# A fused two-block model in fp32: norm sums folded on the way, later tables, and low parts of the normalised tiles made on GpSimd

## What is computed

```python
def rms_norm(x, g):
    y = x * rsqrt(mean(x * x, axis=-1) + EPS)
    return y * g

for l in range(2):                                   # first block
    proj = rms_norm(x, attn_norm[l]) @ w_in[l]
    # three attentions: latent (MLA), differential, chunked
    x = x + concat([o_mla, o_diff, o_ch]) @ w_out[l]
    x = x + conv_ffn(rms_norm(x, ffn_norm[l]), ...)
x = rms_norm(x, final_norm)
h = rms_norm(x, norm_mix_g_2)                        # second block
q, k, v, f, u_ssm, g_attn, g_ssm = split(h @ w_in_2)
x = x + (sigmoid(g_attn) * (y_attn @ w_proj_attn)
         + sigmoid(g_ssm) * (y_ssm @ w_proj_ssm)) @ w_out_2
x = x + hier_moe(rms_norm(x, norm_ffn_g_2), ...)     # 32 experts, two per token
```

## Time and profile before

| | us |
|---|---|
| median of 3 runs | 2308.18 |
| the profiled execution | 2307.2 |
| its span, first to last instruction | 2305.5 |
| PE busy | 2092.2 (91%) |
| DVE busy | 1146.7 (50%) |
| ACT busy | 691.7 (30%) |
| POOL busy | 736.3 (32%) |
| granted TensorE clock, mean share of full speed | 0.965 |

### The profile page before, as it was taken

How to read it: one execution, slowest core, us unless ns; L and a number is a source line. 1 busy time by engine, 2 the same in 40 slices (tenths; PEclk the granted TensorE clock), 3 DMA queues, 4 the chain that set the end, 5 groups by cost and what they waited for, 6 DMA issues and landing times.

```text
span 2305.5 us, 25218 instructions
## 1 busy us (share of the span) xinstructions
PE 2092.2 (91%) x8540; PEld 1339.8 (58%) x8541; DVE 1146.7 (50%) x1929; ACT 691.7 (30%) x1229; POOL 736.3 (32%) x1218
## 2 busy tenths in 40 slices
PE   4999889999797999989999799899998899788795
PEld 3874468888585884466888586346333446333233
DVE  7346756666734436757666833136782522211113
ACT  3227723333412316734333412131000501111010
POOL 4006766656100005766665300001562000111110
PEclk9999999999998999999999999899999998899998
DMA  4210122332232210122323223122321053699984
GB/s 148 92 49 1 37 92 88 113 109 97 70 101 101 92 67 1 38 78 80 117 100 109 72 88 105 37 74 91 110 106 69 27 219 142 243 423 424 425 334 163
DMA packets 43826, 284.19 MB, mean 123 GB/s; under 512 B 8346, under 2 KB 8602, under 8 KB 21072
## 3 DMA queue, kind: packets, MB, share of 16 engines
q1 hardware_dynamic: 33840, 254.34, 29.4%
q0 software_dynamic: 9024, 19.08, 2.2%
q10 hardware_dynamic: 864, 9.44, 1.0%
HBM read 272.68 MB, written 23.60 MB: 129 GB/s over the span
## 4 chain that ended last, share of the span: by engine, by line
PE 77%; DVE 10%; DMA 7%; ACT 3%; POOL 2%; issue 2%; SPq 0%; DVEq 0%; POOLq 0%; ACTq 0%
PE bank L755 10%; PE bank L756 10%; PE bank L757 10%; DMA experts<-in_experts 6%; PE bank L1005 5%; PE bank L1179 4%; PE bank L939 3%; PE bank L940 3%; PE bank L941 3%; PE bank L975 2%; PE bank L1110 2%; PE bank L875 2%; PE bank L742 2%; PE bank L846 2%; PE bank L1182 2%
## 5 line engine op out<-in xcount | busy, mean ns | idle before, releaser
L755 PE MATMUL bank<-h_high,w_high 128*128 128x512 f32 x1056 | 417.7, 396 | 44.5 <-ACT h_high L1426 20.4
L756 PE MATMUL bank<-h_low,w_high 128*128 128x512 f32 x1056 | 415.7, 394 | 0.0
L757 PE MATMUL bank<-h_high,w_low 128*128 128x512 f32 x1056 | 415.5, 393 | 0.0
L1416 ACT ACTIVATE w_high<-extra 128x2048 fp32r<-128x2048 f32 (+1 forms) x104 | 180.5, 1736 | 376.9 <-DVE w_low L1795 376.9
L1792 DVE TENSOR_SCALAR extra<-ring 128x2048 int32<-128x2048 int32 (+1 forms) x104 | 117.8, 1133 | 308.0 <-PE bank L757 182.6
L755 PEld LDWEIGHTS bank<-h_high,w_high 128*128 128x128 f32 x1056 | 201.6, 191 | 94.0 <-issue 36.0
L756 PEld LDWEIGHTS bank<-h_low,w_high 128*128 128x128 f32 x1056 | 201.6, 191 | 41.9
L757 PEld LDWEIGHTS bank<-h_high,w_low 128*128 128x128 f32 x1056 | 201.1, 190 | 42.4
L1795 DVE TENSOR_TENSOR w_low<-ring,extra 128x2048 fp32r<-128x2048 f32 (+1 forms) x104 | 218.6, 2102 | 3.6
L1179 PE MATMUL bank<-experts,rstd 128*64 128x512 f32 x512 | 126.9, 653 | 28.4 <-DMA experts<-in_experts 27.8
L940 PE MATMUL bank<-act_low,w_high 128*128 128x512 f32 x352 | 139.4, 396 | 0.0
(11 more groups left out here) (390 smaller groups left out, 3704.5 us busy)
## 6 DMA issues: line engine op xcount, KB each, us to landing
experts<-in_experts SPq DMA_DIRECT2D x34, 2048.0 KB, 23.5
ring<-in_w_ffn_in SPq DMA_DIRECT2D x44, 1024.0 KB, 4.8
experts<-in_experts SPq DMA_DIRECT2D x34, 1024.0 KB, 21.8
ring<-in_w_ffn_out SPq DMA_DIRECT2D x32, 704.0 KB, 4.1
ring<-in_w_feature SPq DMA_DIRECT2D x14, 1024.0 KB, 4.8
ring<-in_w_rest SPq DMA_DIRECT2D x9, 1024.0 KB, 4.8
ring<-in_w_out SPq DMA_DIRECT2D x8, 1024.0 KB, 4.9
powers_d<-work POOLq DMA_DIRECT2D x16, 512.0 KB, 3.1
```

Source lines behind the costliest of these rows:

```text
L755: pe.matmul(dst, high[:, at], h_high[:, k, :], start=k == 0, stop=False)
L756: pe.matmul(dst, high[:, at], h_low[:, k, :], start=False, stop=False)
L757: return pe.matmul(dst, low[:, at], h_high[:, k, :], start=False, stop=k == KD - 1)
L1416: act.activation(w_high[par_][:, 0:words], w_part[par_][:, 0:words], ACT.Copy).then_inc(w_split, 1)
```

## The change

1. **Sums on the way.** `norm_sum` is one pair of matmuls instead of eight (except for the first norm of all). ACT squares tile m as soon as it has its sum x (`square`), and DVE adds the squares into one tile (`add_square`), during the loop over m of `w_out`, `ffn_out` and `w_out2`.
2. **One seam instead of two at the end of the first block.** The final norm and the norm behind it are computed from two sums, of x^2 and (gain x)^2, taken together; h gets both gains at once, x is multiplied afterwards.
3. **Earlier splits.** The first weight block of the next product is split during the last tiles of the one before (`split_proj(0, l + 1)`, `split(0, 0)`, `split_high(SPLITS, 0)`), and in layer 1 SP loads par and the first weights without waiting for `layer_end`.
4. **Start.** x comes in four parts with four semaphores, weights directly behind it; con2 and rel come later. The S5 angles, sines, factors and the distances move into the feature products of layer 0.
5. **GpSimd.** `lower_tiles` does the subtractions of `split_tile`, 24 in a layer, and stands ahead of the other work of the layer for the first eight, and behind `scale_probs` for the other sixteen; the power tables begin only behind those. The first powers (`first_powers`) come behind the first eight.

```diff
+            def lower_tiles(at):
+                for k in range(KD):
+                    pool.wait_ge(h_masked, at + (k + 1))
+                    pool.tensor_tensor(h_low[:, k, :], h[:, k, :], h_part[:, k, :], ALU.subtract).then_inc(h_lowered, 1)
+                pool.wait_ge(h_lowered, at + KD)
+
             for l in range(LAYERS):
+                lower_tiles(l * (3 * KD))
+                if l == 0:
+                    first_powers()
                 pool.wait_ge(layer_end, l + 1)
...
                 for t in range(NPB):
                     scale_probs(l, t)
+                lower_tiles(l * (3 * KD) + KD)
+                lower_tiles(l * (3 * KD) + 2 * KD)
                 with pool.Fori(l * (ST // LAYERS), (l + 1) * (ST // LAYERS)) as st:
                     power_table(st)
...
                 def split_tile(i, k):
 
-                    at = l * (3 * KD) + (i * KD + k + 1)
                     dve.tensor_scalar(h_part[:, k, :].bitcast(I32), h[:, k, :].bitcast(I32), HIGH_BITS, None, ALU.bitwise_and)\
                        .then_inc(h_masked, 1)
-                    dve.wait_ge(h_masked, at)
-                    dve.tensor_tensor(h_low[:, k, :], h[:, k, :], h_part[:, k, :], ALU.subtract).then_inc(h_lowered, 1)
...
-            sp.dma_start(con2[:], a["con2"]).then_inc(con_in, 16)
...
-            sp.dma_start(x[:], a["x"]).then_inc(x_in, 16)
+            for n in range(X_PARTS):
+                k = KD // X_PARTS
+                sp.dma_start(x[:, n * k:(n + 1) * k, :], a["x"][:, n * k:(n + 1) * k, :]).then_inc(x_in[n], 16)
...
             for l in range(LAYERS):
 
-                sp.wait_ge(layer_end, l + 1)
+                if l:
+                    sp.wait_ge(ffn_act, l * JF)
                 sp.dma_start(par[:], a["par"][l]).then_inc(par_in, 16)
-                sp.dma_start(rel[:], a["rel"][l]).then_inc(par_in, 16)
-                for n in range(FEATURE_BLOCKS):
+                for n in range(RING):
+                    load(l, n, a["w_feature"][l * FEATURE_BLOCKS + n])
+                if l == 0:
+                    sp.dma_start(con2[:], a["con2"]).then_inc(con2_in, 16)
+                sp.dma_start(rel[:], a["rel"][l]).then_inc(rel_in, 16)
+                for n in range(RING, FEATURE_BLOCKS):
...
-            def norm_sum(i, dst, *name):
+            def norm_sum(i, dst, *name, part=0):
 
+                acc, pair = square_tiles(i, part)
+                pe.wait_ge(summed, sums_at(i, KD - 2, part))
+                pe.matmul(dst[:], c("ones"), acc, start=True, stop=False)
+                pe.wait_ge(squares, squares_at(i, KD - 1, part))
+                finish(pe.matmul(dst[:], c("ones"), pair[(KD - 1) % 2], start=False, stop=True), *name)
...
-            norm_sum(2 * LAYERS, bank[7], "norm2", 0)
-            norm_sum(2 * LAYERS + 1, bank[7], "norm2", 1)
+            norm_sum(FINAL, bank[7], "norm2", 0)
+            norm_sum(FINAL, bank[6], "norm2", 1, part=1)
...
+            def square(i, k, part=0):
+                acc, pair = square_tiles(i, part)
+                if k >= 3:
+                    act.wait_ge(summed, sums_at(i, k - 2, part))
+                act.activation(pair[k % 2] if k else acc, x[:, k, :], ACT.Square, scale=c("final_norm", k) if part else 1.0)\
+                   .then_inc(squares, 1)
...
+            act.activation(sum_tiles[0], bank[7][:], ACT.Ln, scale=1.0 / D, bias=c("eps")).then_inc(final_log, 1)
+            act.activation(sum_tiles[1], sum_tiles[0], ACT.Exp, scale=-1.0).then_inc(final_act, 1)
+            act.activation(rstd[:, 1, :], sum_tiles[0], ACT.Exp, scale=-0.5).then_inc(final_act, 1)
+            act.wait_ge(final_step, 1)
+            act.activation(sum_tiles[1], sum_tiles[2], ACT.Ln, scale=1.0 / D, bias=c("eps")).then_inc(final_log, 1)
+            act.activation(sum_tiles[3], sum_tiles[1], ACT.Exp, scale=-0.5).then_inc(final_act, 1)
...
+            def add_square(i, k, part=0):
+                acc, pair = square_tiles(i, part)
+                dve.wait_ge(squares, squares_at(i, k, part))
+                if k >= 2:
+                    dve.wait_ge(summed, sums_at(i, k - 1, part))
+                dve.tensor_tensor(acc, acc, pair[k % 2], ALU.add).then_inc(summed, 1)
...
                     dve.tensor_tensor(x[:, m, :], x[:, m, :], bank[5 + m % 2][:], ALU.add).then_inc(x_added, 1)
+                    if m >= 2:
+                        add_square(l * 2 + 1, m - 1)
+                    if m == 5:
+                        split(0, 0)
...
                 for m in range(KD):
+                    dve.wait_ge(pe_done, done(l, "ffn_half", m))
                     if m + 1 < KD:
-                        dve.wait_ge(pe_done, done(l, "ffn_half", m))
                         split_out(2 * m + 2)
+                    elif l + 1 < LAYERS:
+                        split_proj(0, l + 1)
...
+            dve.wait_ge(final_act, 2)
+            dve.wait_ge(pe_done, done2("norm2", 1))
+            dve.tensor_tensor(sum_tiles[2], bank[6][:], sum_tiles[1], ALU.mult).then_inc(final_step, 1)
+            dve.wait_ge(final_act, 3)
+            dve.tensor_tensor(rstd[:, 0, :], rstd[:, 1, :], sum_tiles[3], ALU.mult).then_inc(final_step, 1)
+            dve.wait_ge(final_step, 2)
+            for k in range(KD):
+                dve.scalar_tensor_tensor(h[:, k, :], x[:, k, :], both_gains[:, k:k + 1], rstd[:, 0, :], ALU.mult, ALU.mult)\
+                   .then_inc(normed, 1)
```

More of the change, by code:

```diff
@@ L411, in build, with square_tiles @@
         act_part += [h[:, n, :] for n in range(KD)] + [conv[0]]
+        sum_tiles = [work[:, (JF + 1 + n) * T:(JF + 2 + n) * T] for n in range(5)]
+        table_tmp = [work[:, (41 + n) * T:(42 + n) * T] for n in range(3)]
+        both_gains = s5[:, 17, 0:KD]
+        def square_tiles(i, part=0):
+            if i == FFN2:
+                return h[:, 0, :], (h[:, 1, :], h[:, 2, :])
+            if part:
+                return rstd[:, 0, :], (sum_tiles[3], sum_tiles[4])
+            return sum_tiles[0], (sum_tiles[1], sum_tiles[2])
         used[0] = 0
@@ L473, in build @@
         pe_done = sem("pe_done")
-        x_in = sem("x_in")
+        x_in = [sem(f"x_in{n}") for n in range(X_PARTS)]
         con_in = sem("con_in")
+        con2_in = sem("con2_in")
+        rel_in = sem("rel_in")
+        summed = sem("summed")
+        final_log = sem("final_log")
+        final_act = sem("final_act")
+        final_step = sem("final_step")
         pos_in = sem("pos_in")
@@ L1503, in _ @@
                     act.activation(h_high[:, k, :], h_part[:, k, :], ACT.Copy).then_inc(h_split, 1)
-                for b in range(2, BLOCKS_OUT):
-                    split_high(BLOCKS_PROJ + b, b % 2)
-                act.wait_ge(pe_done, done(l, "w_out", KD - 1))
-                for k in range(KD):
-                    act.wait_ge(x_added, l * (2 * KD) + (k + 1))
-                    act.activation(h[:, k, :], x[:, k, :], ACT.Square).then_inc(squares, 1)
-                split_high(SPLIT_FFN, 0)
+                for m in range(KD):
+                    if m % 2 and m // 2 + 2 < BLOCKS_OUT:
+                        split_high(BLOCKS_PROJ + m // 2 + 2, m // 2 % 2)
+                    act.wait_ge(x_added, l * (2 * KD) + (m + 1))
+                    square(l * 2 + 1, m)
+                    if m == 5:
+                        split_high(SPLIT_FFN, 0)
                 act.wait_ge(pe_done, done(l, "norm", 1))
@@ L1654, in _ @@
                 act.wait_ge(x_added2, k + 1)
-                act.activation(h[:, k, :], x[:, k, :], ACT.Square).then_inc(squares, 1)
+                square(FFN2, k)
             act.wait_ge(pe_done, done2("norm2", 2))
-            root(2 * LAYERS + 2)
+            root(2 * LAYERS)
             for n in range(2 * NQ):
@@ new lines, in _ @@
+            chain(trig_angle, dve.tensor_scalar(table_tmp[0][:], table_tmp[0][:], c("phase"), None, ALU.add))
+            chain(trig_angle, dve.tensor_scalar(table_tmp[2][:], table_tmp[0][:], math.pi, -TWO_PI, ALU.is_gt, ALU.mult))
+            chain(trig_angle, dve.tensor_tensor(table_tmp[0][:], table_tmp[0][:], table_tmp[2][:], ALU.add))
+            chain(trig_angle, dve.tensor_scalar(table_tmp[0][:], table_tmp[0][:], 3.1415925, -3.1415925, ALU.min, ALU.max))
+            chain(trig_angle, dve.tensor_copy(posc[:], posc_i[:]))
@@ L1753, in _, with signed_sines, distances @@
+            def signed_sines():
+                dve.wait_ge(trig_sin, 1)
+                chain(tables, dve.tensor_scalar(trig[:], trig[:], c("sign"), None, ALU.mult), -12)
+            def distances(i):
                 nk = (i + 1) * P
+                at = P * i * (i + 1) // 2
                 seg = dist[:, at:at + nk]
-                chain(tables, dve.tensor_scalar(seg, tmp[1][:, 0:nk], posc[:, i:i + 1], None, ALU.subtract), -12)
-                chain(tables, dve.tensor_scalar(tmp[2][:, 0:nk], seg, -1.0, None, ALU.mult), -12)
@@ L1855, in _ @@
                     split_proj(n)
+                    if l == 0 and n == 4:
```

(10 more changed lines are left out.)

254 lines of the change are left out of this document (137 added, 117 removed).

## The result

The changed kernel takes 2270.85 us (median of 4 runs, 2269.94 to 2276.85), the kernel before 2307.38 in the same comparison: a ratio of 0.9842, 95% interval 0.9808 to 0.9876, so it is faster by 1.2 to 1.9%. The forecast was 2267. The profiled execution of the changed kernel is its longest of the four, 2276.85 us, with a span of 2275.1.

What follows compares the result with a forecast made beforehand. TensorE, busy 91% of the span, was taken to bound the kernel, with waits at norms where the chain runs over DVE and ACT. 2307.2 - 57.7 + 14.5 + 3.0 = 2267.0 us; range 2252 to 2288.

Steps and rivals of the forecast that it cites:

- Part 1: At start, layer change, FFN norms, first block's end and experts' norm, TensorE's waits shorten: 57.7 us less together.
- mark: At each seam, the end of DVE's first mask on a tile, from which block ends are counted.
- Part 2: At six seams, GpSimd's 48 subtractions take turns with DVE; blocks end at mark + 18.0, costing 14.5 us.
- lower bound: At the six seams, if GpSimd ran freely, blocks would end at mark + 15.4, costing +1 us in all.
- Part 3: Power tables begin after the FFN norm and run beside a stretch of busy DVE: 1.5 us a layer, 3.0 in all.
- 1 (GpSimd free): At the seams, GpSimd's subtractions run freely beside DVE, costing 1.1 instead of 14.5: 2253.6 us; chance 0.08.
- 2 (GpSimd stands back): At six seams, GpSimd yields to queued DVE work or TensorE's clock stays lower; blocks end 4.7 later: 2295; chance 0.10.
- 3: Before layer 1's first subtraction, tables become too slow; 54 us a table gives 2321; chance 0.02.
- 4: At start and seams, late weights or sums give back a third of Part 1, 19 us: 2286; chance 0.04.

Runs made afterwards that it cites:

- the lone subtraction: The changed kernel, but GpSimd begins a seam's subtractions only after DVE has made all 8 masks: 2293.34 us, ratio 0.9938.
- every second one: The changed kernel with every second subtraction (tiles 0, 2, 4, 6) back on DVE, GpSimd keeping the other four of a seam: 2268.27 us, ratio 0.9824.
- GpSimd's parts alone: The kernel before with only the 48 subtractions on GpSimd and the later tables, no seam shortened: 2325.88 us against 2310.12, ratio 1.0065.

## Why the prediction was right, point by point

By its own steps, in the profiled execution:

- Part 1: 57.0 us less, where 57.7 was said. Change of layers 10.9 (10.8), FFN norms 5.4 and 5.4 (10.6 together), end of the first block 19.0 (18.9), experts' norm 3.5 (3.7), start 12.85 (13.7): the weights landed at 15.35 and not at 14.5. That they bind there and not the positions (there at 5.9) was right. So was the nothing for the parts moved into the feature products of layer 0: from the first block's end to the last feature product it is 65.2 us in both kernels. Of the 5.4 at each FFN norm 0.9 isn't the seam's doing: the tables' move alone gives it in the kernel before (10.99 from the last addition to the mark instead of 11.87). Part 1 had this in it without naming it, since it took the mask at 0.42. The matmuls with the matrix of ones go from 56 to 20, which is 36 less and not 42; no term rests on it.
- Part 2: 13.2 where 14.5 was said; block ends at 17.7 to 17.8 where 18.0 was said, pace 2.08 where 2.15 to 2.25 was taken. The mechanism, turns instruction by instruction, is shown by three runs: the lone subtraction (1.25), every second one (only the DVE instruction beside it long), and GpSimd's parts alone (15.8 slower). Only the lower bound is off: six blocks at mark + 15.4 are 0.8 us less than before, not 1 more.
- Part 3: 3.0 was said. `ffn_in` lost nothing (from block end to its last product 228.3 us in all kernels). `ffn_out` lost 0.7 in both layers together in the first profile of the changed kernel (140.57 + 139.26 against 2 x 139.57), 3.6 in the second (142.10 + 140.60), and 2.4 in the kernel before with the tables moved. So the size was about right for what it priced, and `ffn_out` is where it lies. What was missing is the other side. I compared with tables that cost the norms nothing where they lay, but moving them gives back 0.9 at each FFN norm even in the kernel before, so that the move alone costs nothing there that can be measured; and the shortened seam moves the FFN norm under an early table, where the move gains 5.5 us (6.9 and 7.8 at equal clock). It is the better half of what GpSimd's two parts do. The eighth table came 54 us ahead of the next layer's mark (50 said).
- Sum of what was measured in the profiled execution: 2305.5 - 57.0 + 13.2 + 0.7 = 2262.4. What is missing to 2275.1 is 11.0 us in the attentions (layer 0's, less a little in layer 1's) and 1.9 in the second block, within 0.2. The attentions weren't in the prediction at all: in the kernel before, the two had no long low stretch, and I took that for a property of the program.
- Rivals: 1 (GpSimd free) fell, since in one comparison the subtractions on DVE with late tables are 15.0 us faster than the changed kernel (2250.86 against 2265.83; 12.3 at equal clock); 2 (GpSimd stands back) fell: GpSimd's subtractions come in turn with DVE's masks, and at the FFN norm TensorE had full clock from 3.9 us behind its first matmul on. The lower clock did cost time, but in the attentions, where I hadn't looked; 3 and 4 didn't happen.

The median of 10 runs of the changed kernel over both comparisons is 2270.3. So 2267 was right by 0.15%. The mechanism and the two large terms were right; that the error is as small as this is partly luck, since small errors of both signs in the terms and a granted clock that moves one execution against another by up to 27 us were not in the sum.

The version that beats both kernels keeps the shortened seams and late tables and leaves the subtractions on DVE: 2251 to 2252 us, ratios 0.9753 (0.9725 to 0.978) and 0.9739 (0.9705 to 0.9773).

## What to carry to other kernels

Moving an elementwise operation from DVE to GpSimd gained nothing here, where both are in the same chain, and cost 13 us for 48 operations. Elsewhere, look in the trace for a DVE instruction issued just after a GpSimd one and compare its length with that of the same instruction alone. When a seam gets shorter, everything that ran under its old place must be looked up again: background work on GpSimd belongs where DVE waits for the bound engine, not under a norm. And before a gain of 1% is read from medians, compare the same stretches of several profiles, and put each execution's time beside its mean granted clock.

## What the runs showed that was not expected

- The same 12.50 us of attention, 72 matmuls busy 12.04 us, were followed once by 47.8 us at a granted clock of 0.5 and once by full clock, in one kernel; this long stretch begins 95.5 us behind the last feature product both times, and costs 14 us. What decides it, and whether the change makes it more frequent, stays open: no run was made on it.
- In its second half TensorE is busy 24.30 of 24.30 us, so a low clock can look like a fully used engine.
- GpSimd operations on 128 or 256 elements, not only wide ones, stretch DVE's: a mask takes 0.62 or 0.83 instead of 0.42, and a subtraction 0.83 or 1.11 instead of 0.69.
- Tiles that arrive faster don't end a block sooner than TensorE's own 13 us behind its first matmul; begun at mark + 8.5 it ended at + 21.4.
